# Head means of an encoder layer's projections: squares split into a high and a low part before they meet the mean matrix

## What is computed

```python
def _rmsnorm(x, g):
    xf = x.astype(jnp.float32)
    y = xf * lax.rsqrt(jnp.mean(xf * xf, axis=-1, keepdims=True) + EPS)
    return (y * g.astype(jnp.float32)).astype(x.dtype)

def _layer(x, ...):
    B, L = x.shape[0], x.shape[1]
    h = _rmsnorm(x, norm1_g)
    proj = h @ w_in
    qa, ka, va, qb, kb, vb = jnp.split(proj, SPLITS, axis=-1)
    qa = _rmsnorm(qa.reshape(B, L, NA_HEADS, HEAD_DIM), qn_a_g)
    ka = _rmsnorm(ka.reshape(B, L, NA_HEADS, HEAD_DIM), kn_a_g)
    ...
    qb = _rmsnorm(qb.reshape(B, L, WG_HEADS, HEAD_DIM), qn_b_g)
    kb = _rmsnorm(kb.reshape(B, L, WG_KV_HEADS, HEAD_DIM), kn_b_g)
```

## Time and profile before

| | us |
|---|---|
| median of 3 runs | 1989.07 |
| lowest, highest | 1988.44, 1994.43 |
| span of the profiled execution | 1992.9 |
| PE busy in it | 1868.3 (94%) |
| DVE, ACT, POOL busy | 1301.1, 996.6, 951.9 |
| projection of segment 0 | about 42 to 165 |
| projection of segment 1 | about 187 to 308 |
| projection of segment 2 | about 526 to 643 |

### The profile page before, as it was taken

How to read it: one execution, slowest core, us unless ns; L and a number is a source line. 1 busy time by engine, 2 the same in 40 slices (tenths; PEclk the granted TensorE clock), 3 DMA queues, 4 the chain that set the end, 5 groups by cost and what they waited for, 6 DMA issues and landing times.

```text
span 1992.9 us, 35832 instructions
## 1 busy us (share of the span) xinstructions
PE 1868.3 (94%) x12047; PEld 1678.4 (84%) x12047; DVE 1301.1 (65%) x2349; ACT 996.6 (50%) x2069; POOL 951.9 (48%) x807
## 2 busy tenths in 40 slices
PE   5995998999699997997899999999999999999998
PEld 3795777999577885887899999899999989999997
DVE  2566657888465886548666666776666676666664
ACT  3354346888435784336454443535444363544432
POOL 1331335765234652114464554646465564646553
PEclk9997998999799898998999999999999999999999
DMA  4442622444422445011332323253233325323321
GB/s 118 134 142 77 160 78 74 115 127 135 106 84 83 135 138 207 22 63 43 127 106 84 123 87 105 85 191 106 84 111 100 105 86 190 106 84 109 102 84 64
DMA packets 178796, 213.33 MB, mean 107 GB/s; under 512 B 12980, under 2 KB 157860, under 8 KB 178700
## 3 DMA queue, kind: packets, MB, share of 16 engines
q1 hardware_dynamic: 178700, 212.10, 34.2%
HBM read 195.76 MB, written 25.18 MB: 111 GB/s over the span
## 4 chain that ended last, share of the span: by engine, by line
PE 56%; DVE 5%; ACT 2%; issue 2%; POOL 1%; DMA 0%; ACTq 0%; POOLq 0%; DVEq 0%; SPq 0%
PE bank L384 18%; PE bank L385 18%; PE bank L386 18%; DVE mvl L1826 1%; POOL msl L1061 1%; ACT msh L1349 0%; DVE qm L1725 0%; DVE tsum L1822 0%; ACT logit L1275 0%; ACT qm L1299 0%; DVE pmeta L1676 0%; DVE logit L1661 0%; DVE ptl L1668 0%; PE bank L2092 0%; PE bank L2070 0%
## 5 line engine op out<-in xcount | busy, mean ns | idle before, releaser
L384 PE MATMUL bank<-mvh,sth 128*128 128x256 f32 x1848 | 526.7, 285 | 17.4 <-DVE act_f L1842 5.6
L385 PE MATMUL bank<-mvl,sth 128*128 128x256 f32 x1848 | 525.7, 284 | 0.0
L386 PE MATMUL bank<-mvh,stl 128*128 128x256 f32 x1848 | 525.5, 284 | 0.0
L384 PEld LDWEIGHTS bank<-mvh,sth 128*128 128x128 f32 x1848 | 357.5, 193 | 20.5 <-issue 16.7
L385 PEld LDWEIGHTS bank<-mvl,sth 128*128 128x128 f32 x1848 | 357.5, 193 | 1.2
L386 PEld LDWEIGHTS bank<-mvh,stl 128*128 128x128 f32 x1848 | 357.4, 193 | 0.0
L1131 POOL TENSOR_TENSOR dl<-draw,dh 128x1024 fp32r<-128x1024 f32 x66 | 157.9, 2415 | 369.3 <-ACT dh L1442 369.3
L1864 DVE TENSOR_TENSOR y<-bank,y 128x512 f32<-128x512 f32 x264 | 182.4, 691 | 166.9 <-PE bank L386 166.1
L995 POOL TENSOR_TENSOR wl<-wraw,wh 128x1024 fp32r<-128x1024 f32 x54 | 132.6, 2457 | 277.4 <-ACT wh L1186 277.4
L1125 POOL TENSOR_TENSOR stl<-graw,sth 128x512 fp32r<-128x512 f32 x132 | 177.2, 1343 | 102.4 <-ACT sth L1424 98.2
L384 PE MATMUL bank<-dh,acth 128*128 128x512 f32 x528 | 210.8, 399 | 7.7 <-DVE y L1864 5.3
(11 more groups left out here) (239 smaller groups left out, 4251.8 us busy)
## 6 DMA issues: line engine op xcount, KB each, us to landing
graw<-in_w_gate SPq DMA_DIRECT2D x33, 1024.0 KB, 5.4
uraw<-in_w_up SPq DMA_DIRECT2D x33, 1024.0 KB, 5.4
draw<-in_w_down SPq DMA_DIRECT2D x66, 512.0 KB, 4.3
wraw<-in_w_in SPq DMA_DIRECT2D x54, 512.0 KB, 3.9
bias_rows<-table_a SPq DMA_DIRECT2D x36, 192.0 KB, 3.1
out<-y SPq DMA_DIRECT2D x12, 512.0 KB, 3.3
bias<-table_b SPq DMA_DIRECT2D x28, 201.0 KB, 2.6
table_a<-line_a_dram SPq DMA_DIRECT2D x8, 576.0 KB
```

Of the source, the lines that this page charges most:

```text
L384: pe.matmul(out, lhs[0], rhs[0], start=start, stop=False, skip_group_check=True)
L385: pe.matmul(out, lhs[0], rhs[1], start=False, stop=False, skip_group_check=True)
L386: return pe.matmul(out, lhs[1], rhs[0], start=False, stop=stop, skip_group_check=True)
```

## The change

Ahead of each head mean the square is split as the other operands are. ACT copies it to fp32r (`sqh`, new L1249), after waiting for its own square; POOL subtracts the copy from the square (`sql`, new L1023, in place of the square); PE waits for `squared_lo`, which POOL signals, and makes two products with `head_mean_r`, an fp32r copy of the matrix that DVE rounds once at the start. PE no longer waits for `squared`. The scratch output of `norm_root` moves to another address, at the same size.

```diff
     head_mean = r("head_mean", [P, P])
+    head_mean_r = at("head_mean_r", [P, P], F32R, r.offset - P * 4)
...
+        sqh_of.append([s(f"sqh_{n}{i}", [P, SEG + META], F32R) for i in range(2)])
+        sql_of.append([at(f"sql_{n}{i}", [P, SEG + META], F32R, where + i * 4 * (SEG + META)) for i in range(2)])
...
+        def squares_split(g, kind):
+            return ([sqh_kv], [sql_kv]) if g and kind == "kvb" else (sqh_of[g // 2], sql_of[g // 2])
+
+        def square_columns(g, kind):
+            return SEG + META if g == 0 and kind != "q" else SEG
...
                 def body(it, kind, i):
-                    if kind != "kvb":
-                        weight_lo(it + 1)
+                    w = square_columns(g, kind)
+                    sq = squares(g, kind)[0]
+                    sqh, sql = squares_split(g, kind)
+                    for slot in range(2):
+                        if kind != "kvb":
+                            weight_lo_of(it + 1, slot)
+                        if kind == "q" or slot == 0:
+                            pool.wait_ge(squared_hi, normed_number(g, kind, slot, i) + 1)
+                            pool.tensor_tensor(sql[slot][:, 0:w], sq[slot][:, 0:w],
+                                               f32(sqh[slot][:, 0:w]), ALU.subtract).then_inc(squared_lo, 1)
...
                             op.then_inc(squared, 1)
+                            act.wait_ge(squared, j0 + slot + 1)
+                            w = square_columns(g, kind)
+                            act.activation(squares_split(g, kind)[0][slot][:, 0:w], sq[slot][:, 0:w], ACT.Copy
+                                           ).then_inc(squared_hi, 1)
...
                         j = normed_number(g, kind, slot, i)
-                        pe.wait_ge(squared, j + 1)
+                        pe.wait_ge(squared_lo, j + 1)
...
                         for u0, w, _, mb in units(g, kind, slot):
-                            op = pe.matmul(mb[:, 0:w], head_mean[:, :], sq[slot][:, u0:u0 + w],
-                                           start=True, stop=True)
+                            pe.matmul(mb[:, 0:w], head_mean_r[:, :], sqh[slot][:, u0:u0 + w],
+                                      start=True, stop=False, skip_group_check=True)
+                            op = pe.matmul(mb[:, 0:w], head_mean_r[:, :], sql[slot][:, u0:u0 + w],
+                                           start=False, stop=True, skip_group_check=True)
```

More of the change, by code:

```diff
@@ L150, in hybrid_encoder_layer @@
     assert BASE + s.offset <= END
-    junk1 = [at("junk1p", [P, D], F32, qm_at[2] + 4 * (SEG + META) * 4), at("junk1s", [P, D], F32, tmp)]
-    sq_of, rt_of = [], []
+    junk1 = [spare[:, 0:2, SEG:2 * SEG], at("junk1s", [P, D], F32, tmp)[:, :].rearrange("p (a b) -> p a b", a=2)]
+    sq_of, sqh_of, sql_of, rt_of = [], [], [], []
     for n, where in (("p", qm_at[2]), ("s", v_at + 4 * 1280 * 4)):
@@ L275, in hybrid_encoder_layer @@
         squared = sem("squared")
+        squared_hi = sem("squared_hi")
+        squared_lo = sem("squared_lo")
         v_copied = sem("v_copied")
@@ L991, in project, with weight_lo_of @@
             def project(g):
+                def weight_lo_of(it, slot):
+                    pool.wait_ge(w_hi, 18 * g + it * 2 + slot + 1)
+                    pool.tensor_tensor(wl[slot][:, :, :], wraw[slot][:, :, :], f32(wh[slot][:, :, :]),
+                                       ALU.subtract).then_inc(w_lo, 1)
                 def weight_lo(it):
                     for slot in range(2):
-                        pool.wait_ge(w_hi, 18 * g + it * 2 + slot + 1)
-                        pool.tensor_tensor(wl[slot][:, :, :], wraw[slot][:, :, :], f32(wh[slot][:, :, :]),
-                                           ALU.subtract).then_inc(w_lo, 1)
+                        weight_lo_of(it, slot)
                 def body(it, kind, i):
-                    if kind != "kvb":
-                        weight_lo(it + 1)
+                    w = square_columns(g, kind)
[8 more added lines that the diff above has]
+                                               f32(sqh[slot][:, 0:w]), ALU.subtract).then_inc(squared_lo, 1)
                 weight_lo(0)
@@ L1154, in norm_root @@
                 wait(act, ss_done, m)
-                act.activation(junk1[g // 2][0:rows, :], xt[g][m % 3][0:rows, :], ACT.Square,
+                act.activation(junk1[g // 2][0:rows], xt[g][m % 3][0:rows, :].rearrange("p (a b) -> p a b", a=2), ACT.Square,
                                accum_out=ssq[0:rows, m:m + 1]).then_inc(ss_done, 1)
@@ L2001, in after @@
                 def after(kind, i, slot, first=False):
-                    sq = squares(g, kind)[0]
+                    sqh, sql = squares_split(g, kind)
                     if kind == "q" or slot == 0:
                         j = normed_number(g, kind, slot, i)
-                        pe.wait_ge(squared, j + 1)
+                        pe.wait_ge(squared_lo, j + 1)
                         if not (first and g == 0):
```

3 lines of the change are left out of this document (added).

## The result

The changed kernel takes 2022.28 us (median of 5 runs, 2020.35 to 2024.12), the kernel before 1991.0 beside it (5 runs): 1.0154 times the time, 95% interval 1.0144 to 1.0165, so 31 us more. Forecast were 2017 and 28 us more, range 2005 to 2027. The profiled execution of the changed kernel spans 2020.9 us, 28.0 more than the one before.

What follows compares the result with a forecast made beforehand. PE, busy 94% of the span, was taken as the bound. 14.4 us off against new waits gave +20.9, with 6.8 for the clock +27.7, added to the median 1989.1: 2017 us, range 2005 to 2027.

Steps and rivals of the forecast that it cites:

- What the change takes away: Head means where PE is the bound: two fp32r products save 0.40 us a mean, 36 means, 14.4 us off.
- Keys and values, second to fourth pair: Nine means in three segments: PE waits 2.59, 2.47 and 1.77 us for POOL's subtraction behind the weights, 20.5 us on.
- waits of PE for `wl` ahead of its products: Sign of a wrong forecast: POOL's new work delays the weights too, which was counted at nothing.
- First pair of keys, last pair of segment 0: Three first means of keys: 2.13 us each, 6.4 us on; segment 0's last pair, 528 columns: 2.2 us on.
- First mean of segment 0: Segment 0's start: square's low part between POOL's two weight blocks, partly hidden by the low clock, net 1.4 us on.
- Queries: Second to fourth pair, slot 0, nine means: PE waits 0.14 to 0.64 us, taken as 0.42, 3.8 us on.
- Starts of attention: POOL's subtraction ahead of the first queries' low parts: 0.2 us in segment 1, 0.8 in segment 2, 1.0 on.
- The clock: Nine new long waits may bring 1.2 GHz, 1.7 us lost each; four falls taken, 6.8 us on.
- The rival that the clock holds: Clock holds at all new waits: +20.9 us, 2008 to 2013; chance 0.24.
- The rival of 2024 to 2029: Clock falls nearly every time, and POOL and DVE collide in the queries: 2024 to 2029 us; chance 0.12.

Runs made afterwards that it cites:

- the waits alone: Changed kernel with copy, subtraction and PE's wait kept, but each mean again one fp32 product, of the high part: 2036.6 us, ratio 1.0221 to the kernel before.
- the kernel with PE kept at work: Changed kernel plus 8 (segment 2: 6) extra fp32r products ahead of PE's wait in pairs of keys and values: 2009.54 us, ratio 1.0084 to the kernel before.
- the two other kernels that have the same waits: Changed kernel with one fp32 product per mean, 2036.6 us; kernel before with only the 15 means of keys split, 2025.29 us.

## Why the prediction held, and where it was off

The forecast lies in the right place for the reason that it gives: a third step on POOL, in line behind the weights, and the clock behind the waits. That it comes within 5 us owes something to luck, as terms that were too high and one that was too low cancel in part.

**What the change takes away.** A pair of fp32r products does cost 0.46 us: 84.60 - 84.37 = 0.23 from the one to the other. Mean and 24 products in a stream took 6.41 us on average (6.42 in the earlier trace rows); without POOL's step they take 6.04. That is 0.37 us a mean, not 0.40, and the waits alone show 0.38: 13.5 us at 36 means for the term of 14.4.

**Keys and values, second to fourth pair.** The mechanism is as foreseen, event by event. Waits of 1.9 to 2.3 us were measured as idle time in segments 0 and 1 and 1.3 to 1.6 in segment 2, against 2.5 and 1.8 worked out from start to start (a record's end includes the array's 0.17 us or so, which hides from the idle figure). The rest of the surplus is POOL's 1.29 in place of 1.34 us and signals that are shorter than I gave them. That PE is the bound in these loops too was a wrong reading. The idle column shows no wait, but in segments 0 and 1 the kernel before lost about 0.3 us a round behind the third and the fourth mean, waiting for POOL's weights (279.55 above). That wait is gone once the mean itself comes after the weights, so the forecast, which counted the whole new wait as added, had these rounds too high. In the kernel with PE kept at work, where the clock held, the way from the first mean of keys to the last is 7.1, 5.2 and 3.6 us longer than before in the three segments, 15.9 in all, against 17.9 by the forecast's terms (20.5 + 2.2 - 12 x 0.40): 2 us less. The sign named for a wrong forecast, waits of PE for `wl` ahead of its products, did not appear in the loops of the changed kernel.

**First pair of keys, last pair of segment 0.** 0.66 us of idleness became 2.64, and 2.53 became 4.59: 2.0 and 2.1 on top, against 2.13 and 2.2.

**First mean of segment 0.** The shift at the second mean is 59.67 - 58.23 = 1.44 us, forecast 1.4.

**Queries.** The step on POOL and DVE was mis-sized. I left open who gets through first and took 0.42 us (the upper bound of 0.64 has no source in my rows; 0.14 and the 0.36 by which the weights were longer beside DVE make 0.50). POOL did, and DVE was the one held up:

```profile
89.10 1.31 POOL L1023 TENSOR_TENSOR sql_p<-sq_p,sqh_p 128x512 fp32r<-128x512 f32 x1
...
89.31 1.65 DVE L1630 SCALAR_TENSOR_TENSOR qm<-raw,gains,rt_p 128x512 f32 x1 [0.17 <-DVE rt_p L1620]
```

DVE's product lasts 1.65 us in place of 0.75, and nobody misses it. PE waits the lower bound of 0.14 us, and then loses 0.10 more, as the second product follows the first after 0.33 us and not 0.23:

```profile
90.17 0.40 PE L393 MATMUL bank<-hth,wl 128*128 128x512 f32 x1
90.54 0.49 PE L2045 MATMUL bank<-sqh_p,head_mean_r 128*128 128x512 f32 x1
90.87 0.39 PE L2047 MATMUL bank<-sql_p,head_mean_r 128*128 128x512 f32 x1
```

Together 0.24 us at nine means, 2.2 us against 3.8.

**Starts of attention.** POOL finished `sql_kv` and went on to the first queries, as said. The table gives segment 2 +6.0 us from its first mean of keys to the first maximum; the forecast's terms there, without the clock, are -1.6 + 5.3 + 0.8 = 4.5, and one fall of the clock makes up the rest. From the last mean (640.60 and 670.09) to that maximum the shift grows by 0.7 us, the start's own 0.8. In segment 1 it shrinks by 0.2, from the last mean (304.87 and 329.24) to PE's second scores, where I had 0.2 on.

**The clock.** This is the term that was mis-sized most: four falls assumed, eight came. They cost 12.7 us (the experiment that kept PE at work), against 6.8. The rival that the clock holds is out; its 2008 to 2013 is what that experiment measured, where the clock did hold. The rival of 2024 to 2029 had the falls right and the collision in the queries wrong. Why such a wait brings the clock down at one place and not at another is not settled: it fell behind eight, six and seven of the nine waits in three kernels, 21 of 27, and the place where it held was not the same.

The sum again with what was measured: 27.7 + 5.9 for the clock, - 1.6 for the waits of the queries, + 0.7 for the smaller gain at 23 means of queries, - 2 for the keys gives 31, against 31; the terms are not known so well that this would mean more than a closed account. In the profiled pair 2.2 us came off in the later stages, where the change does nothing; single executions differ by that.

## What to carry to other kernels

When the operands of a small product are split to make it cheaper on PE, ask first which queue the split enters, and what stands in that queue at the moment the product is wanted; here a 1.3 us subtraction for each mean, in the loops over keys behind one of 2.5 to 2.8 us, cost 37 us with all that followed, where the cheaper products are worth some 13.5. A split can still pay where the queue has room: done for the queries alone it made the kernel 5.8 us faster. A stream without idle marks can still be waiting: compare the distances of the same two instructions in two rounds. And price a new wait of two or more us on PE with the clock behind it; in this kernel a fall cost 1.6 us and came behind about three waits in four.

## What was not expected of the hardware

More work made the changed kernel faster: 88 extra fp32r products in PE's waits took 12.7 us off, as the granted clock then stayed at 1.00. In the changed kernel, waits of 1.3 to 1.6 us left the clock alone in all three cases, and those of 1.9 to 2.7 us at the keys brought it down in eight of nine; with the two other kernels that have the same waits it is none of nine and 21 of 27.

The Trainium skill ("SBUF — State Buffer", section "SBUF: two separate sides") says that a DVE operation with two SBUF inputs and a POOL operation that reads SBUF exclude each other for a whole instruction, and whichever starts first goes through. In the queries POOL began at 89.10 and DVE at 89.31, and DVE ended 0.55 us after POOL did (90.96 and 90.41), so the trace agrees, and the price fell on the engine that could bear it.
